# Sparse experts for 64 more tokens: 352 tokens dense instead of 384, 192 index-picked rows of each table instead of 160

## The reference

```
q = (xb @ w_q).reshape(n, 8, 2, 128)
s = einsum('nhpc,hpkc->nhpk', q, sub_keys)
v1, i1 = top_k(s[:, :, 0], 16); v2, i2 = top_k(s[:, :, 1], 16)
best, sel = top_k(v1[..., :, None] + v2[..., None, :], 16)   # over the 256 pairs
eidx = i1 * 128 + i2 at sel;  gate = softmax(best)
hid = gelu(einsum('nd,nhkd->nhk', xb, u_tab[eidx]))
out = einsum('nhk,nhkd->nd', gate * hid, v_tab[eidx])
```

## Time and profile before

| | us |
|---|---|
| median of 3 runs (5028.31 to 5032.72) | 5031.31 |
| the profiled execution, own time | 5025.87 |
| span of its trace | 5024.3 |
| TensorE busy, share of span | 98% |
| VectorE busy, share of span | 62% |
| ScalarE, GpSimd busy, share of span | 32%, 14% |

### The profile page before, as it was taken

How to read it: one execution, slowest core, us unless ns; L and a number is a source line. 1 busy time by engine, 2 the same in 40 slices (tenths; PEclk the granted TensorE clock), 3 DMA queues, 4 the chain that set the end, 5 groups by cost and what they waited for, 6 DMA issues and landing times.

```text
span 5024.3 us, 83155 instructions
## 1 busy us (share of the span) xinstructions
PE 4917.6 (98%) x35827; PEld 4767.0 (95%) x35827; DVE 3129.6 (62%) x3935; ACT 1600.2 (32%) x1769; POOL 706.1 (14%) x606
## 2 busy tenths in 40 slices
PE   8999999999999999999899999999999999999998
PEld 7999999999999999989899999999999999999998
DVE  6555544444555343223489989987666677777777
ACT  4444323323444222122222234443222222222222
POOL 0000000000000000000000033333332222222221
PEclk9999999999999999999999999999999999999999
DMA  6422232223333432231322378988888899989995
GB/s 250 161 99 105 98 100 83 83 81 126 107 117 128 140 112 85 85 108 68 120 102 101 112 296 340 340 336 332 339 325 306 327 339 328 329 328 335 333 329 206
DMA packets 263067, 1010.01 MB, mean 201 GB/s; under 512 B 47760, under 2 KB 127760, under 8 KB 176784
## 3 DMA queue, kind: packets, MB, share of 16 engines
q1 hardware_dynamic: 177840, 547.93, 31.0%
q0 software_dynamic: 68832, 442.58, 23.3%
q10 hardware_dynamic: 16128, 15.60, 0.9%
HBM read 918.77 MB, written 87.24 MB: 200 GB/s over the span
## 4 chain that ended last, share of the span: by engine, by line
PE 76%; DVE 13%; DMA 6%; issue 2%; DVEq 2%; ACT 1%; POOL 1%; ACTq 0%; SPq 0%; PEldq 0%; POOLq 0%
PE psum L1328 20%; PE psum L941 13%; PE psum L1138 12%; PE psum L1250 10%; PE psum L912 7%; PE psum L1155 4%; DMA arena<-in_u,eidx 3%; DVE e_lo L2169 3%; DMA tmp<-in_u,eidx 1%; PE psum L889 1%; DVE arena L2334 1%; DVE tmp L2334 1%; DVE tmp L2363 1%; PE psum L873 1%; DVE tmp L2358 1%
## 5 line engine op out<-in xcount | busy, mean ns | idle before, releaser
L2169 DVE TENSOR_TENSOR e_lo<-ring,e_hi 128x2048 fp32r<-128x2048 f32 x270 | 618.9, 2292 | 319.7 <-ACT e_hi L1616 305.8
L1616 ACT ACTIVATE e_hi<-ring 128x2048 fp32r<-128x2048 f32 x270 | 517.7, 1918 | 799.4 <-PE psum L1328 650.3
L1250 PE MATMUL psum<-h_hi,e_hi 128*128 128x384 f32 x2032 | 696.0, 343 | 24.7 <-DVE e_lo L2169 24.6
L1328 PE MATMUL psum<-c_hi,e_hi 128*128 128x384 f32 x2048 | 685.6, 335 | 7.4 <-issue 3.7
L1250 PE MATMUL psum<-h_hi,e_lo 128*128 128x384 f32 x2048 | 689.5, 337 | 0.0
L1250 PE MATMUL psum<-h_lo,e_hi 128*128 128x384 f32 x2032 | 686.0, 338 | 0.0
L1328 PE MATMUL psum<-c_lo,e_hi 128*128 128x384 f32 x2048 | 684.3, 334 | 0.0
L1328 PE MATMUL psum<-c_hi,e_lo 128*128 128x384 f32 x2048 | 684.3, 334 | 0.0
L941 PE MATMUL psum<-p_hi,e_lo 128*128 128x272 f32 x1792 | 518.1, 289 | 0.0
L1250 PEld LDWEIGHTS psum<-h_hi,e_hi 128*128 128x128 f32 x2032 | 382.9, 188 | 29.8 <-DVE e_lo L2169 15.9
L1328 PEld LDWEIGHTS psum<-c_hi,e_hi 128*128 128x128 f32 x2048 | 384.4, 188 | 12.6 <-issue 9.4
(11 more groups left out here) (476 smaller groups left out, 10326.4 us busy)
## 6 DMA issues: line engine op xcount, KB each, us to landing
ring<-in_weights SPq DMA_DIRECT2D x200, 1024.0 KB, 4.9
ring<-in_uT SPq DMA_DIRECT2D x128, 1024.0 KB, 6.6
ring<-in_v SPq DMA_DIRECT2D x128, 1024.0 KB, 8.7
hid<-tmp POOLq DMA_DIRECT2D x128, 192.0 KB, 6.7
gates<-arena POOLq DMA_DIRECT2D x12, 2048.0 KB, 12.9
arena<-hid SPq DMA_DIRECT2D x32, 768.0 KB, 10.4
arena<-gates SPq DMA_DIRECT2D x32, 768.0 KB, 14.8
gate_in<-tmp ACTq DMA_DIRECT2D x64, 136.0 KB, 4.6
```

What stands on the lines that cost most here:

```text
L1250: mm = nc.tensor.matmul(psum[:, 2 + r % 2, 0:ND], w, h[:, c, 0:ND], start=(c == 0 and i == 0), stop=(c == KD - 1 and i == 2))
L1328: mm = nc.tensor.matmul(psum[:, d, 0:ND], w, c[p // 2][:, 2 * (p % 2) + r, :], start=(first and r == 0 and j == 0), stop=(last and r == 1 ...
L1616: nc.scalar.activation(hi_slot(n, reg), e_raw[n % R], ACT.Copy).then_inc(w_rounded, 1)
L2169: nc.vector.tensor_tensor(e_lo[n % R], e_raw[n % R], as_f32(hi_slot(n, reg)), ALU.subtract)\
```

## The change

EXTRA goes from 32 to 64, so ND goes from 384 to 352, PICKS from 160 to 192, and each extra pick holds two slots (SIDES = 2) of 64 tokens instead of four slots of 32. NGT goes from 12 to 11 and ROW_D from 72 to 68: there are 44 rows with gate steps, with 73 picks, and the remaining 113 picks (192 - 6 - 73) are spread over rows 68 to 121. TensorE's loop over the gate rows takes eight rows at a time, so its last four are written out. The rest follows: sizes of tiles, a place for `coef_t`, four small index and gate moves instead of eight, two PSUM banks for the extra sums.

```diff
-TAIL, EXTRA = 128, 32
+TAIL, EXTRA = 128, 64
+SIDES = P // EXTRA
 T_AT = NT - TAIL
 ND = T_AT - EXTRA
 PICKS = TAIL + EXTRA
...
-        coef_t, e = view(arena, e, 1, PICKS)
+        coef_t, _ = view(tmp, TMP_N - 2 * HN - PICKS, 1, PICKS)
...
-            for n in range(4):
+            for n in range(SIDES):
                 rows_n, cols_n = slice(EXTRA * n, EXTRA * (n + 1)), slice(EXTRA * n, EXTRA * (n + 1))
                 pool.dma_start(eidx_x[rows_n, :], x_idx[:, cols_n]).then_inc(pk["x_in"], 16)
-                pool.dma_start(gate_t[rows_n, TAIL:PICKS], slots[0:NS, 2, Q_EXTRA, cols_n]).then_inc(pk["x_in"], 16)
+                pool.dma_start(gate_t[rows_n, TAIL:PICKS], slots[0:EXTRA, 2, Q_EXTRA, cols_n]).then_inc(pk["x_in"], 16)
...
                 if k == TAIL:
-                    pool.wait_ge(pk["x_in"], 16 * 8)
+                    pool.wait_ge(pk["x_in"], 32 * SIDES)
...
-                    rows = P if q < 4 else NS
+                    rows = P if q < 4 else EXTRA
...
+            for q in range(4 * (NGT % 2)):
+                r = ROW_D - 4 + q
+                row_tile(r + 16, r)
+                for g in range(2):
+                    gate_step(2 * (r - ROW_C) + g)
             with pe.Fori(0, (NKEY - ROW_D) // 4) as i:
...
-                mm = nc.tensor.matmul(psum[:, 4, k * EXTRA:(k + 1) * EXTRA], ytok_x[:, k * P:(k + 1) * P], cst("fold"),
+                mm = nc.tensor.matmul(psum[:, 4 + k // 8, k % 8 * EXTRA:(k % 8 + 1) * EXTRA], ytok_x[:, k * P:(k + 1) * P], cst("fold"),
...
-                    mm = nc.tensor.matmul(psum[:, 5, 0:PICKS], ones, tail_sq[:, 4 * c + k, :],
+                    mm = nc.tensor.matmul(psum[:, 7, 0:PICKS], ones, tail_sq[:, 4 * c + k, :],
...
-                    four = [P, KD, 4, EXTRA]
-                    nc.vector.tensor_tensor(hx.rearrange("p k (s n) -> p k s n", s=4),
+                    four = [P, KD, SIDES, EXTRA]
+                    nc.vector.tensor_tensor(hx.rearrange("p k (s n) -> p k s n", s=SIDES),
...
-            nc.vector.tensor_tensor(dst, dst, psum[:, 4, :].rearrange("p (k n) -> p k n", k=KD), ALU.add)
+            nc.vector.tensor_tensor(dst, dst, psum[:, 4:6, :].rearrange("p b (k n) -> p (b k) n", k=8), ALU.add)
...
-    put("fold", np.tile(np.eye(EXTRA), (4, 1)))
+    put("fold", np.tile(np.eye(EXTRA), (SIDES, 1)))
```

More of the change, by code:

```diff
@@ L473, in program @@
         skT, e = view(arena, 3 * D, 2 * HEADS, NKEY)
+        coef_t, _ = view(tmp, TMP_N - 2 * HN - PICKS, 1, PICKS)
+        assert 2 * ND + 4 * QUAD * ND <= TMP_N - 2 * HN - PICKS
         gate_t, e = view(arena, e, 1, PICKS)
         hid_t, e = view(arena, e, 1, PICKS)
-        coef_t, e = view(arena, e, 1, PICKS)
         gate_t, hid_t, coef_t = gate_t[:, 0, :], hid_t[:, 0, :], coef_t[:, 0, :]
@@ L501, in program @@
               "keys_in qs s sev top gexp sl slT slTe eq g gev gfree hTp hTe idx x_in".split()}
-        x_idx = selu[0:NS].rearrange("p a q n -> p (a q n)")[:, 0:P]
-        eidx_x = tiu[:, 0, 0:EXTRA]
+        x_idx = selu[0:EXTRA].rearrange("p a q n -> p (a q n)")[:, 0:P]
+        eidx_x = tiu[:, 0:2, :].rearrange("p q n -> p (q n)")
         hid, e = view(tmp, 0, 2, ND)
@@ L1342, in _ @@
             pair_tiles(8 * N_BLOCKS - 4, True, True, N_BLOCKS)
-            pe.wait_ge(y_free, 8 * N_BLOCKS + 13)
+            pe.wait_ge(y_free, 8 * N_BLOCKS + 14)
             pe.wait_ge(tail_sum, EXTRA)
             for k in range(KD):
-                mm = nc.tensor.matmul(psum[:, 4, k * EXTRA:(k + 1) * EXTRA], ytok_x[:, k * P:(k + 1) * P], cst("fold"),
+                mm = nc.tensor.matmul(psum[:, 4 + k // 8, k % 8 * EXTRA:(k % 8 + 1) * EXTRA], ytok_x[:, k * P:(k + 1) * P], cst("fold"),
                                       start=True, stop=True)
@@ L1740, in _ @@
             act.wait_ge(pk["idx"], 1)
-            act.wait_ge(pk["x_in"], 16 * 8)
+            act.wait_ge(pk["x_in"], 32 * SIDES)
             act.sem_inc(pk["gfree"], 4)
@@ L1802, in _ @@
             act.wait_ge(ss_ready, SUMS["final"] + 1)
-            nc.scalar.activation(flat_root[:, ND:NT], psum[:, 5, 0:PICKS], ACT.Sqrt, bias=eps, scale=1.0 / D)\
+            nc.scalar.activation(flat_root[:, ND:NT], psum[:, 7, 0:PICKS], ACT.Sqrt, bias=eps, scale=1.0 / D)\
                 .then_inc(root_ready, 1)
@@ L2207, in tiles @@
             def tiles(buf, lo, hi):
-                return [buf[0:P if q < 4 else NS, q, lo:hi] for q in range(QT)]
+                return [buf[0:P if q < 4 else EXTRA, q, lo:hi] for q in range(QT)]
             def top_keys(i, step):
@@ L2213, in top_keys @@
                 bank = 4 + 2 * half
-                scores = [psum[:, bank, q * P:(q + 1) * P] for q in range(4)] + [last[0:NS, :]]
+                scores = [psum[:, bank, q * P:(q + 1) * P] for q in range(4)] + [last[0:EXTRA, :]]
                 rest = tiles(work, 0, NKEY)
@@ L2220, in top_keys @@
                 dve.wait_ge(pk["s"], i * 2 + (step + 1))
-                nc.vector.tensor_copy(scores[4], psum[0:NS, bank + 1, 0:P])
+                nc.vector.tensor_copy(scores[4], psum[0:EXTRA, bank + 1, 0:P])
                 dve.drain()
@@ L2239, in candidates @@
                 nc.vector.tensor_copy(tif[:, 0:4, :], tiu[:, 0:4, :])
-                nc.vector.tensor_copy(tif[0:NS, 4, :], tiu[0:NS, 4, :])
+                nc.vector.tensor_copy(tif[0:EXTRA, 4, :], tiu[0:EXTRA, 4, :])
                 four = [P, QT, TOPK, TOPK]
@@ L2319, in _ @@
                                            in1=slots[:, 1, Q_TAIL, :], op0=ALU.mult, op1=ALU.add)
-            nc.vector.scalar_tensor_tensor(out=coef_t[0:NS, 0:P], in0=slots[0:NS, 0, Q_EXTRA, :], scalar=float(NKEY),
-                                           in1=slots[0:NS, 1, Q_EXTRA, :], op0=ALU.mult, op1=ALU.add)
+            nc.vector.scalar_tensor_tensor(out=coef_t[0:EXTRA, 0:P], in0=slots[0:EXTRA, 0, Q_EXTRA, :], scalar=float(NKEY),
+                                           in1=slots[0:EXTRA, 1, Q_EXTRA, :], op0=ALU.mult, op1=ALU.add)
             nc.vector.tensor_copy(gate_t[:, 0:TAIL], slots[:, 2, Q_TAIL, :])
@@ L2324, in _ @@
             nc.vector.tensor_copy(eidx[:, :], hid_t[:, 0:TAIL])
-            nc.vector.tensor_copy(x_idx, coef_t[0:NS, 0:P])
+            nc.vector.tensor_copy(x_idx, coef_t[0:EXTRA, 0:P])
             dve.drain().then_inc(pk["idx"], 1)
@@ L2392, in _ @@
                     dve.wait_ge(hid_act, 1)
-                    dve.wait_ge(pk["x_in"], 16 * 8)
+                    dve.wait_ge(pk["x_in"], 32 * SIDES)
                     nc.vector.tensor_tensor(coef_t, hid_t, gate_t, ALU.mult)
```

## The result

The changed kernel takes 5111.31 us (median of four runs, 5098.78 to 5129.38), the kernel before 5029.84 beside it (four runs, 5028.31 to 5032.72): ratio 1.0162, 95% interval 1.0147 to 1.0178. It is slower by some 81 us, where 69 had been forecast, inside the range and on the forecast side. The profiled execution is the slowest of the four, own time 5129.38, span 5127.8, so in its rows the loss is 103.5 us (span against span); the median run lost some 20 us less, and no trace shows in which stage.

What follows compares the result with a forecast made beforehand. VectorE plus late picks bounds gate rows, TensorE late rows and v tiles, with picks and DMA thinly covered. Terms -2 - 41.4 + 161.5 - 4 - 47 + 2 = +69 us on the median 5031.3 give 5100 us, range 5020 to 5165.

Steps and rivals of the forecast that it cites:

- Rows up to 23: Rows 0 to 23: VectorE's search keeps its time, TensorE's faster rows return a little; -2 us.
- Gate rows: Rows with gate steps, 44 instead of 48: VectorE's pace plus late picks stays, 455.7 us, or -41.4 us.
- 10.36 us a row stays: Rows with gate steps: same picks and VectorE work per row, so narrower matmuls leave the time per row unchanged.
- Late rows: Rows after the gate steps: two buffers limit 113 picks to 5.2 us each, 582.4 us against 420.95; +161.5 us.
- my upper bound of 5.44: Rows after the gate steps: slowest time per pick in us, an estimate from median landings; it gives +188 us.
- After the last dot: From the last dot to the end of the rows: 50.4 us become 46.4, by faster TensorE rows; -4 us.
- v tiles: v part: 8.0 us a tile, between TensorE's 7.72 and 8.27 from the stage's DMA rate scaled to full share; -47 us.
- End: Products with `fold`, sums of squares and the tail's vector work get more columns or elements; +2 us.
- the picks keep up: Rival, late rows: shorter landings, 4.4 us a pick, and full v gain, 4977 us; 14 in 100 with all-hidden case.
- The v part gives nothing: Rival, v tiles: TensorE waits for DMA at about its old 8.386 us a tile, 5147 us; 17 in 100.
- The rival of the clock: Rival, late rows: TensorE idles, its clock stays low, rows take 14.1 us, up to 170 us more; 7 in 100.
- `hid` of row 127: Sign in the profile after: this write comes about 115 us later after row 24's first dot.

Runs made afterwards that it cites:

- the run with wide rows: Changed kernel with only the matmuls of the 128 rows of u widened back from 352 to 384 columns: 5121.15 us, ratio 1.0176.
- the run with the drain: Changed kernel with VectorE waiting after each late dot until GpSimd, drained after every pick's issue, signals the next pick issued: 5848.02 us, ratio 1.1624.
- the runs with three and four buffers: Changed kernel with three or four instead of two buffers for picks of u from row 68 on: 4998.47 us with three, 4950.47 us with four.

## Why the prediction was right

- **Rows up to 23: -2 forecast, -0.6 measured** (first dot of row 24 at 2942.01, before 2942.65).
- **Gate rows: -41.4 forecast, -30.8 measured** (497.1 to 466.3 us for 48 and 44 rows). The step "10.36 us a row stays" was a little low: 10.60. VectorE's waits for picks are 42.7 us in 44 rows of the changed kernel, and 31.6 in the run with wide rows, whose gate rows take 454.7 us (their window stands with that run). That is nearly the whole difference of 11.6 us. It is no accident of one run: with five picks in three rows and 352 columns five traces have 462.4 to 466.3 us (the run with the drain aside), with 384 columns two have 454.1 and 454.7. Why narrower matmuls make these picks later was not tried.
- **Late rows: +161.5 forecast, +201.2 measured.** The mechanism was right, as the runs with three and four buffers show; the term was too small. I took 5.2 us a pick out of 5.0 to 5.4, and it was 5.555, above my upper bound of 5.44. That bound rested on medians of landing. What counts in a loop is the mean of the landings on its chain, and there a long one such as 8.94 mostly follows each short one such as 7.63. In the changed kernel the 66 late picks that VectorE waited for took 8.48 us on average (median 7.89), which gives (2.57 + 8.48) / 2 = 5.53 us a pick. The number could have been had ahead: in the trace before, the 39 such picks took 8.54, and (2.57 + 8.54) / 2 = 5.55. Why every other landing is long was not looked into.
- **After the last dot: -4 forecast, -2.3 measured** (50.4 to 48.1 us, to `row_out` at 4078.58).
- **v tiles: -47 forecast, -65.1 measured** (1080.6 to 1015.5 us up to the products with `fold`). The tile of 8.0 us was a middle between TensorE's 7.72 and a DMA bound of 8.27; at 7.81 it came out near the first, as the window of the earlier trace rows had it (7.80) and the scaled stage had not. Both engines are full there, TensorE at 938 of 948 us and DMA at a share of 1.00; without the 32 picks a tile is 7.69 at a share of 0.92. At 7.81 all 128 tiles would give -74 us; the 9 us between lie at the start and the end of the v tiles and were not looked into.
- **End: +2 forecast, +1.0 measured.**

Together +103.5 us in the spans, 34 more than forecast. The misses are +40 in the late rows, +11 in the gate rows and -18 in the v tiles; that they partly cancel is luck. The median run, with its loss of 81 us, came within 12 of the forecast. The mechanism and the sign of every term were right.

Of the rivals, "the picks keep up" fell with 5.555 us a pick, where 4.6 would have decided. "The v part gives nothing" fell with 7.81 us a tile, and with the 72 us that wide products in the v part cost. The Trainium skill, "DMA: Bandwidth & Descriptors", section Specifications, gives 358 GB/s from HBM for a core, as half of a stack's 716; taken as the ceiling of the one core that runs here it would have had it so, and 386 GB/s over 934 us measures otherwise. Its 435 GB/s for the fabric is not contradicted: 421 was the most that a stage here held. The rival of the clock was right in the symptom alone. TensorE's timeline in a late row:

```profile
3595.19 0.51 PE L1252 MATMUL psum<-h_hi,e_hi 128*128 128x352 f32 x1 [3.62 <-DVE e_lo L2176]
3595.50 0.50 PE L1252 MATMUL psum<-h_lo,e_hi 128*128 128x352 f32 x1
...
3599.56 0.32 PE L1252 MATMUL psum<-h_hi,e_lo 128*128 128x352 f32 x1
3599.72 0.32 PE L1252 MATMUL psum<-h_hi,e_hi 128*128 128x352 f32 x1
```

After 3.62 us without work the matmuls come 0.3 us apart, 1.2 in place of 2.4 GHz, and by 3599.56 they are 0.16 apart again; the stage's granted clock is 0.88. TensorE waits for picks anyway, so this costs nothing, as the wide rows showed with still more TensorE work in the same time.

Of the signs named ahead, `hid` of row 127 was put too low: it came 168 us later after row 24's first dot (1136.6 against 968.4 us), not 115, by the terms of the gate rows and the late rows above.

## What to carry to other kernels

A loop that fetches into few buffers has a pace of its own: (time from the start of the work on a buffer to the issue into it + mean time from issue to landing) divided by the buffers. Work it out before more fetches are traded for less arithmetic, and look for room that has come free by then: here two buffers more turned a loss of 81 us into a gain of 76, and were worth nothing as long as TensorE set the pace. Take the landing as the mean over the picks that were waited for, not as a median over all. The landing is no constant when buffers are added: it rose from a median of 7.5 to 7.7 us with two buffers to 11.4 to 12.8 with four, as the DMA engines filled up.

## What was not expected of the hardware

- The 16 DMA engines held 421 GB/s over 430 us of 8 KB rows by index and 1 MB loads, and 386 GB/s with many packets under 2 KB.
- The issue of an indirect DMA on GpSimd was 0.96 us alone and mostly 2.74 to 2.92 beside VectorE's `split_e` of 128x2048 elements, but about 0.96 beside its one-hots. By the trace a semaphore increment behind it went off before it ran, and a drain behind it took some 5 us.
- With narrower matmuls the gate rows were 8 to 12 us longer (462.4 to 466.3 in five traces, 454.1 and 454.7 with wide rows). In the two traces compared, the waits for picks make up the difference; the cause is open.
